# A decoder layer with a product-key expert FFN: 42 instead of 32 tokens take the gathered path, whole expert rows are gathered, and the low weight parts are shared out anew

## What is computed

```python
s = einsum('thpd,hpkd->thpk', (xn @ w_pq).reshape(T, 8, 2, 128), sub_keys)
# per token and head: the best 16 of 128 x 128 product keys -> experts, gates (8 x 16 = 128 per token)
act = gelu(einsum('tkd,td->tk', expert_u[experts], xn))       # 128 experts of 16384 for each token
y   = einsum('tk,tkd->td', gates * act, expert_v[experts])
out = rmsnorm(x2 + y, final_norm_gain)
```

## Time and profile before

| what | value |
|---|---|
| median of 3 runs (lowest, highest) | 1914.57 us (1914.4, 1914.7) |
| profiled execution, first to last instruction | 1912.2 us, 2.4 us below the median of the launches |
| PE, PEld busy | 1896.7 us, 1758.9 us |
| VectorE, ACT, GpSimd busy | 1383.4 us, 950.5 us, 1390.8 us |
| u pieces run from about | 571 us to 1251 us |
| v pieces run from about | 1251 us to 1899 us |
| DMA | 448.29 MB, mean 234 GB/s |
| TensorE's granted clock | 0.997 of full speed |

### The profile page before, as it was taken

The page is one execution under the profiler, slowest core; times in us unless marked ns, Lnnn a source line. Parts: engine busy times, 40 slices in busy tenths (PEclk is TensorE's granted clock), DMA queues, the critical chain, the costliest instruction groups (busy, mean ns, idle before and its releaser), DMA issues.

```text
span 1912.2 us, 35061 instructions
## 1 busy us (share of the span) xinstructions
PE 1896.7 (99%) x11798; PEld 1758.9 (92%) x11798; DVE 1383.4 (72%) x2585; ACT 950.5 (50%) x1342; POOL 1390.8 (73%) x708
## 2 busy tenths in 40 slices
PE   9999999999999999999999999999999999999997
PEld 7888889888999999999999999999999999999997
DVE  7534684045545777968888888479889889999986
ACT  6453355475544444544444444455555555555555
POOL 3867768887998999998888888976555525666711
PEclk9999999999999999999999999999999999999999
DMA  8544546564655666666666566689999988999984
GB/s 307 186 143 153 199 144 224 193 190 155 218 188 177 207 209 208 210 202 196 194 192 196 189 195 195 200 280 351 333 336 334 333 297 298 337 325 334 328 273 145
DMA packets 128380, 448.29 MB, mean 234 GB/s; under 512 B 16528, under 2 KB 19472, under 8 KB 127632
## 3 DMA queue, kind: packets, MB, share of 16 engines
q1 hardware_dynamic: 102240, 367.29, 58.5%
q0 software_dynamic: 20480, 67.13, 10.0%
q10 hardware_dynamic: 5584, 12.88, 2.0%
HBM read 443.04 MB, written 4.19 MB: 234 GB/s over the span
## 4 chain that ended last, share of the span: by engine, by line
PE 72%; POOL 17%; issue 8%; DMA 1%; DVE 1%; ACT 0%; POOLq 0%; SPq 0%; DVEq 0%; ACTq 0%
PE ps L1885 22%; PE ps L1982 22%; POOL wlo L438 17%; PE ps L1888 12%; PE ps L1985 11%; PE ps L1899 1%; PE ps L1585 1%; PE ps L1587 1%; PE ps L1586 1%; PE ps L1961 1%; DMA raw<-in_w_front 0%; PE ps L1869 0%; DMA big<-in_x_t 0%; PE ps L1963 0%; ACT whi L539 0%
## 5 line engine op out<-in xcount | busy, mean ns | idle before, releaser
L438 POOL TENSOR_TENSOR wlo<-raw,whi 128x1024 fp32r<-128x1024 f32 x436 | 1057.6, 2430 | 207.9 <-ACT whi L539 193.1
L539 ACT ACTIVATE whi<-raw 128x1024 fp32r<-128x1024 f32 x435 | 461.2, 1060 | 633.7 <-PE ps L1888 361.8
L1885 PE MATMUL ps<-x_parts,whi 128*128 128x448 f32 x2048 | 588.9, 369 | 0.0
L1982 PE MATMUL ps<-gate_parts,whi 128*128 128x448 f32 x1992 | 573.6, 369 | 0.0
L734 ACT ACTIVATE whi<-raw 128x1024 fp32r<-128x1024 f32 x256 | 271.7, 1061 | 294.9 <-PE ps L1985 255.8
L1888 PEld LDWEIGHTS ps<-x_parts,wlo 128*128 128x128 f32 x2048 | 384.7, 188 | 31.3
L1985 PEld LDWEIGHTS ps<-gate_parts,wlo 128*128 128x128 f32 x1992 | 374.2, 188 | 30.8
L1888 PE MATMUL ps<-x_parts,wlo 128*128 128x224 f32 x2048 | 386.9, 270 | 0.0
L1985 PE MATMUL ps<-gate_parts,wlo 128*128 128x224 f32 x1992 | 376.0, 270 | 0.0
L1437 DVE TENSOR_TENSOR wlo<-raw,whi 128x1024 fp32r<-128x1024 f32 x248 | 303.9, 1225 | 68.1 <-ACT whi L734 52.1
L1885 PEld LDWEIGHTS ps<-x_parts,whi 128*128 128x128 f32 x2048 | 310.3, 191 | 0.0
(11 more groups left out here) (266 smaller groups left out, 2217.2 us busy)
## 6 DMA issues: line engine op xcount, KB each, us to landing
raw<-in_w_u SPq DMA_DIRECT2D x256, 512.0 KB
raw<-in_w_v SPq DMA_DIRECT2D x256, 512.0 KB
raw<-in_w_front SPq DMA_DIRECT2D x180, 512.0 KB
big<-in_mem ACTq DMA_DIRECT2D x8, 256.0 KB, 5.6
big<-in_mem_t ACTq DMA_DIRECT2D x2, 1024.0 KB, 6.2
big<-in_x ACTq DMA_DIRECT2D x2, 1024.0 KB, 7.3
x_back<-x2t_scratch ACTq DMA_DIRECT2D x2, 896.0 KB
big<-in_x_t SPq DMA_DIRECT2D x3, 512.0 KB, 8.4
```

Of the source, the lines that this page charges most:

```text
L438: nc.gpsimd.tensor_tensor(wlo[:, j % SPL, :], raw[:, j % RAW, :], whi[:, j % SPL, :], ALU.subtract).then_inc(lo_done, 1)
L539: nc.scalar.activation(whi[:, j % SPL, :], raw[:, j % RAW, :], ACT.Copy).then_inc(hi_done, 1)
L1885: nc.tensor.matmul(sums[:, 0:2 * TD], whi[:, s, cols], x_parts[:, :, m, 0:TD], start=m == 0, stop=False, skip_group_check=True)
L1982: nc.tensor.matmul(sums[:, 0:2 * TD], whi[:, s, cols], gate_parts[:, g, :, 0:TD], start=False, stop=False, skip_group_check=True)
```

## The change

TS becomes 42 and TD 214. The partitions hold three groups of 42 tokens; a token's 128 experts are split into three lists of up to 43 (PER), and each gather fetches 128 whole rows of 8 KB: 43 gathers of u and 43 of v, into a ring of three, one per 2.47 v pieces. VectorE takes each with one instruction over 2048 elements. The three groups' sums are put together at the end by SBUF DMAs to the first 42 partitions and three adds; `FOLD` is gone. In u, VectorE takes the low part of one piece in twelve; in v, GpSimd takes the first eight and then every even piece.

```diff
-TD, TS, PARTS, PD = 224, 32, 4, 512
+GROUPS = 3
+TS = P // GROUPS
+TD = T - TS
+PER = -(-P // GROUPS)
-RING = 12
+RING = 3
-def taken_u(d):
-    return 15 + d * 41 // 50
-def taken_v(e):
-    return 132 + e * 21 // 25
+ROWS_FROM, WEIGHTS_AT_PIECE, ROWS_UNTIL = 15, 127, 234
+ADDED_AT = (*range(240, 239 + GROUPS), 251)
+def taken(n):
+    if n < PER:
+        return ROWS_FROM + n * (WEIGHTS_AT_PIECE - 6 - ROWS_FROM) // PER
+    return WEIGHTS_AT_PIECE + 1 + (n - PER) * (ROWS_UNTIL - WEIGHTS_AT_PIECE) // PER
+def issued(n):
+    return 3 + n if n < RING else taken(n - RING) + 2
...
+            with pool.Fori(U0 // BODY, U0 // BODY + U_BODIES) as i:
+                for j in range(BODY):
+                    if j != U_VECTOR:
+                        rest_of(i * BODY, j)
...
+            for j in range(2 * NK):
+                if j < OPENING or j >= BODY and j % 2 == 0:
+                    rest_of_v(j)
+                if j == 3:
                     pool.wait_ge(picks, 1)
+                while asked < 2 * PER and j >= issued(asked):
+                    gather(asked)
+                    asked += 1
...
+                if j == 3:
+                    for g in range(GROUPS):
+                        act.dma_start(X_S[g * TS:(g + 1) * TS, :], x2_dram).then_inc(x_s_in, 16)
+                if j == 6:
+                    act.dma_start(X_GAINED, gain_rows[0].partition_broadcast(P)).then_inc(gain_s_in, 16)
...
                 nc.vector.reduce_sum(LATE[:, c % ACT_BANKS, :] if late else W[:, k0 + c, :], sums, AX).then_inc(sums_joined, 1)
+                if c % CHUNKS_PER_BODY == U_VECTOR // 2 - 2:
+                    n = 2 * c + 4
+                    dve.wait_ge(hi_done, k0 * 2 + (U0 + n + 1))
+                    nc.vector.tensor_tensor(wlo[:, (U0 + n) % SPL, :], raw[:, n % RAW, :], whi[:, (U0 + n) % SPL, :],
+                                            ALU.subtract).then_inc(lo_u_done, 1)
...
-                v_step(j, split=V0 + j >= POOL_END)
+                v_step(j, split=OPENING <= j < BODY or j > BODY and j % 2 == 1)
...
-            for k, src in enumerate((CH[:, 0, last], CH[:, 1, last], GE[:, last], stats[:, R + N_X2 + 1:R + N_X2 + 2])):
-                w = P if k < 3 else 1
-                ins = nc.tensor.matmul(ps[:, 7, k * P:k * P + w], SEL, src, start=True, stop=True)
+            for k, src in enumerate((CH[:, 0, last], CH[:, 1, last], GE[:, last])):
+                for g in range(GROUPS):
+                    w = min(PER, P - g * PER)
+                    nc.tensor.matmul(ps[:, 7, k * PER:k * PER + w], SEL[:, g, :], src[:, g * PER:g * PER + w],
+                                     start=g == 0, stop=g == GROUPS - 1, skip_group_check=True)
+            for g in range(GROUPS):
+                ins = nc.tensor.matmul(ps[:, 7, 3 * PER:3 * PER + 1], SEL[:, g, :], stats[:, R + N_X2 + 1:R + N_X2 + 2],
+                                       start=g == 0, stop=g == GROUPS - 1)
...
-                if j == 1:
-                    pe.wait_ge(rows_taken, P)
-                    for b in range(2):
-                        ins = nc.tensor.matmul(ps[:, b, 2 * TD:512], FOLD, SUMS[:, b * 64:(b + 1) * 64],
-                                               start=False, stop=False, skip_group_check=True)
```

More of the change, by code:

```diff
@@ L495, in _, with rest_of_v @@
-            assert asked == [P, P]
+            with pool.Fori(U0 // BODY, U0 // BODY + U_BODIES) as i:
+                for j in range(BODY):
+                    if j != U_VECTOR:
+                        rest_of(i * BODY, j)
+            for j in range(RAW):
+                rest_of(U0 + U_BODIES * BODY, j)
+            def rest_of_v(j):
+                pool.wait_ge(hi_done, V0 + j + 1)
+                k = (V0 + j) % SPL
+                nc.gpsimd.tensor_tensor(wlo[:, k, :], raw[:, j % RAW, :], whi[:, k, :], ALU.subtract).then_inc(lo_done, 1)
@@ L788, in _ @@
             for j in range(BODY):
+                high_v((LAST_BODY - 1) * BODY, j)
+                gated_high((LAST_BODY - 1) * BODY - NK, j)
+                if j == 8:
+                    act.wait_ge(rows_taken, 2 * PER)
+                    load_addend(0)
+                    load_addend(1)
+            for j in range(BODY):
                 high_v(LAST_BODY * BODY, j)
@@ L1426, in _ @@
                     gate_step(i, j)
-            left = TOK_PAIRS - full * PAIRS_PER_BODY
-            for j in range(left):
-                gate_step(full, j, TOK_PAIRS)
-            joins_done = C_GATE + full * CHUNKS_PER_BODY + left // 2
+            for j in range(BODY):
+                gate_step(full, j, TOK_PAIRS - full * PAIRS_PER_BODY)
+            joins_done = C_GATE + (full + 1) * CHUNKS_PER_BODY
             takes_done = joins_done - 2
@@ L1949, in _ @@
                 u_piece(first + full, j)
-                if j < left:
-                    gate_products(full, j)
-            assert first + full + 1 == 2 * NK // BODY
-            for j in range(2 * NK - 2 * NK // BODY * BODY):
-                u_piece(2 * NK // BODY, j)
+                if j % 6 < 5 and j - j // 6 < left:
+                    gate_products(full, j - j // 6)
+            for i in range(first + full + 1, U_BODIES):
+                for j in range(BODY):
+                    u_piece(i, j)
+            for j in range(RAW):
+                u_piece(U_BODIES, j)
             def v_block(s, c, first=False, last=False):
@@ L2228 @@
                                              a["cross_norm_gain"][0], a["ffn_norm_gain"][0], a["final_norm_gain"])]
-    part, token = i // TS, i % TS
-    sparse = np.concatenate([i[:, None] == T - P + (token - TS)[None, :], token[:, None] == token[None, :],
-                             part[:, None], (part // 2 * 2 * P * NK + part % 2)[:, None]], 1)
+    sparse = np.stack([(i[None, :] // TS == g) & (i[:, None] == P - TS + i[None, :] % TS) for g in range(GROUPS)], 1).reshape(P, -1)
     arrays = {
@@ L2244 @@
         "c_inv": inv.astype(np.float32)[None],
-        "u_rows": a["peer_u"][0].reshape(-1, PD), "c_sparse": sparse.astype(np.float32),
+        "u_rows": a["peer_u"][0], "v_rows": a["peer_v"][0], "c_sparse": sparse.astype(np.float32),
     }
```

345 lines of the change are left out of this document (165 added, 180 removed).

## The result

The changed kernel takes **2061.8 us** (median of 4 runs, 2059.8 to 2066.5), the kernel before 1914.6 in the same session: 1.077 times as long, 95% interval 1.0758 to 1.0789. The prediction said 1889 and no more than 1918. The profiled execution has a span of 2060.8 us where it had 1912.2.

What follows compares the result with a forecast made beforehand. PE's own rate was taken to bound u and v, whi matmuls by streaming and wlo by weight loads. Terms from -36 for narrower matmuls summed to -25.7 us, giving 1889 us; forecast 1880 to 1898, range 1866 to 1918.

Steps and rivals of the forecast that it cites:

- Narrower matmuls: PE in u and v: 214 columns for 224 shorten whi pairs, wlo pairs stay; 2.45 us per piece, -36 us.
- rival of shrinking wlo pairs: PE's wlo matmuls shrink with their columns too, saving another 19 us: 1870 us; chance 12%.
- unchanged whi pairs: Rival: whi matmuls keep their 0.42 us at 428 columns, none of the 36 us comes back: 1925 us; chance 3%.
- Steady v, compute: VectorE's 4.85 us and GpSimd's 4.3 us of work per row fit in PE's 6.04 us: covered, 0.
- Steady v, DMA: Loads and gathers in v ask for 388 GB/s, against a ceiling taken as 400: +3 us, bounds 0 and +53.
- a little short: Rival in v: DMA at 375 GB/s makes a piece take 2.53 us: 1903 us; chance 12%.
- the bound of v: Rival in pieces 15 to 234: DMA lands data more slowly than PE uses it, 1939 us at 352 GB/s; chance 13%.
- GpSimd in u: VectorE takes one low part in twelve to keep GpSimd at pace; its extra work costs +0.3 us, bounds 0 and 2.5.
- Opening of v: First pieces of v: three gathers ahead of GpSimd's low parts cost +3.5 us, the DMA traffic behind them +1.5.
- The test that the prediction set: Prediction is wrong if v takes longer per piece than u without gates, or VectorE's rows make PE wait.
- the third and fourth rival: Slower cases: DMA becomes the bound of v (13%), and whi matmuls gain nothing from fewer columns (3%).

Runs made afterwards that it cites:

- experiment 12: Changed kernel with GpSimd's v low parts from piece 12 written as zeros, every second gather left out, all u low parts on GpSimd: 1893.2 us.
- experiment 5: Changed kernel with GpSimd's v low parts from piece 12 written as zeros and every second gather from the third row on left out: 1904.3 us.
- experiment 3: Changed kernel with GpSimd writing zeros in place of its low parts of v from piece 12 on: 1929.1 us.
- experiments 1: Changed kernel with all of v's low parts from piece 8 on made by VectorE: 1947.0 us, 1.017 times the kernel before.
- 2: Changed kernel with GpSimd making every fourth low part of v from piece 12 on, not every second: 1995.9 us.
- experiment 8: Changed kernel with v's low parts from piece 8 on VectorE and all of u's on GpSimd: 1934.9 us, 1.0112 times the kernel before.
- experiment 9: As experiment 8, but VectorE takes one u low part in twelve before the gates, and v's opening gathers and copies are spread out: 1939.0 us.
- experiment 6: Changed kernel with VectorE's gate part in v computed as a scaling of one SBUF input, not a difference of two: 2039.8 us.
- experiment 7: Changed kernel with VectorE's gate part in v computed as a reduction over one element, with one SBUF input: 2016.9 us.
- experiment 4: Kernel before the change with only the split added, GpSimd making v's even low parts from piece 12 on: 2037.7 us.

## Why the prediction was wrong

Four kernels, each differing from the next by one thing, split the 173 us between the forecast and the result. The order matters: with the lock in place the share of DMA is not to be seen.

| from | to | us | what it is |
|---|---|---|---|
| 1889 (forecast) | 1893.2 (experiment 12) | 4 | opening and small terms |
| 1893.2 | 1904.3 (experiment 5) | 11 | VectorE's low part in u |
| 1904.3 | 1929.1 (experiment 3) | 25 | DMA in steady v |
| 1929.1 | 2061.8 (the change) | 133 | the lock in steady v |

Experiments 12, 5 and 3 ran once. The same u took 672 us in the profiled executions of experiments 1 and 3 and 678 in those of 2, 5 and the change, so the rows with 11, 25 and 133 may each be off by 6, and 11 is rather 8 (u took 8.4 us less in experiment 8 than in 1, 13.5 less in 12 than in 5, of which 6 may be that scatter); the large one is not in doubt.

- *Narrower matmuls* was right. The timeline of PE in u after the change, two pairs of each kind:

```profile
901.21 0.56 PE L1936 MATMUL ps<-x_parts,whi 128*128 128x428 f32 x2
...
901.61 0.38 PE L1939 MATMUL ps<-x_parts,wlo 128*128 128x214 f32 x2
...
901.83 0.56 PE L1936 MATMUL ps<-x_parts,whi 128*128 128x428 f32 x2
...
902.23 0.37 PE L1939 MATMUL ps<-x_parts,wlo 128*128 128x214 f32 x2
```

  A unit takes 0.62 us (901.21 to 901.83). Whi pairs take 0.40 us (0.42 in the earlier trace rows) and wlo pairs stay at 0.21 to 0.22; where nothing waits a piece takes 2.44 us (experiment 5) for the 2.45 predicted. The rival of shrinking wlo pairs and that of unchanged whi pairs fall.
- *Steady v, compute: "4.85 us of work in 6.04 ... GpSimd has ... 4.3 us. Covered, 0"* is **the step that failed**. It set each engine's time against PE's by itself. The times add: 4.85 + 3.0 for GpSimd's low parts is 7.85, more than 6.04; measured are 7.5 (3.06 x 2.465). GpSimd's idle time was taken for free, and while VectorE reads two inputs from SBUF it is not. It cost 133 us where 0 stood. The row of before that shows it (1253.82, above) stood in the stretch that the prediction read for GpSimd's pace. It was passed over because PE lost nothing there: GpSimd's 2.49 us were the pace anyway, and a gate part of 2.49 fitted in it. A slip beside it cost nothing: 4.9 less 1.1 and 1.6 is 2.2, which does not cover a row's 2.4 us, but in experiment 5 PE kept 2.44 us per piece with all rows in VectorE's queue.
- *Steady v, DMA*: +3, measured 25. The demand of 388 GB/s was worked out rightly, and the engines nearly reach it: over the 200 us that take 2.58 us per piece they move 368 GB/s at a share of 0.95. The 400 GB/s that the prediction took for the ceiling is not one for a short time (experiment 9: 430 over 1273 to 1277). That it is bursts of 1 MB beside loads four deep that keep the mean lower is likely, but not shown. Both DMA rivals come close: 2.58 lies past "a little short" (2.53) and at the edge of "the bound of v" (2.585). In the changed kernel none of this was seen, since the lock had slowed the demand to 309 GB/s.
- *GpSimd in u: "I give this +0.3"*: measured about 8. The step looked for VectorE being late in the choice of experts, not beside the gates, where its low part pushes the next gates' work back, once in twelve pieces. Its premise, GpSimd too slow at 2.49, was wrong as well (2.40 for one, and PE's pace kept in experiment 8). So u gained nothing: its last piece began at 1249 us in both kernels.
- *Opening of v*: +5, measured about 7 (pieces 3 to 6 took 3.5, 3.5, 6.0 and 3.8 us). The count of 10 MB at 400 GB/s had no place for the stretch at 175.
- The test that the prediction set, "wrong if v takes longer per piece than u without gates, or if VectorE's rows make PE wait", is what came. None of its rivals was the case in the changed kernel: each was about one engine or one queue against PE, none about two engines against each other. (Its chances also have a slip: the third and fourth rival, named as the slower ones, add up to 0.16, not 0.14.)

The Trainium skill has the rule: its page "SBUF — State Buffer", section "Who interferes with whom", says that VectorE and GpSimd share a pair of SBUF ports, locked for a whole instruction, that a VectorE instruction with two SBUF inputs contends with a GpSimd instruction that reads SBUF and not with one that only writes, and that the modes of doubled rate over two ports contend too, a reduction never. What it says of who waits for whom is what the traces show: 371 against 2527 ns, the zeros (377 against 382 ns), the scaling (260 against 2416 ns) and the reduction (364 against 365 ns). That ports are the reason no run shows. The prediction weighed rules of other pages; this is the one that speaks against the change.
The Trainium skill's page "DMA: Bandwidth & Descriptors" gives in its specifications about 358 GB/s of HBM per core. The 372 GB/s over 100 us in experiment 3 are over that, and yet the rival that the figure stood beside, DMA as a bound of v, holds in a milder form.

**Can the change pay?** Not as it stands, by these runs. With the low parts divided as in the kernel before and the schedule spread, it comes to 1924, 0.7% slower than before. What 42 tokens take from PE comes back as waits for DMA in steady v (2.56 us per piece for 2.45) and as a stop of 5 us or more in its opening. How much VectorE adds, which is busy nine tenths of the time there, was not separated. The kernel before stays the fastest that was run, of those that compute everything.

## What to carry to other kernels

Before work is moved to an idle engine, ask what it shares with the busy one: add the times of VectorE's instructions with two SBUF inputs and of GpSimd's instructions that read SBUF as if they were one engine, and compare that sum with the pace. A VectorE instruction of one input at the doubled rate counts too (experiment 6), a reduction does not (experiment 7). Count each engine's own load as well: in experiment 4 GpSimd's gathers and low parts filled it. In a trace the mark is an instruction whose duration has two values, the longer of which ends a fixed time after the other engine's; look at single instances in the timeline, since a group's mean (441 ns for the gate parts of the whole kernel before, 385 for the steady ones) shows it only as a small excess. And when a bound is removed, expect the next one right behind it: DMA, invisible at 3.06 us per piece, was worth 25 us at 2.58. And compare a pace with an engine's busy time in a stretch rather than with a sum of durations, which overlap here by 0.08 us each.
